# Norm products, a router constant and the first gathers in a two-layer hybrid trunk with experts

## What is computed

```python
sh1, sc1, ga1, sh2, sc2, ga2 = adaln(c, w_mod[l], b_mod[l])
p = modulated_norm(xs, g_norm1[l], sh1, sc1) @ w_in[l]
...
xs = xs + ga1 * (jnp.concatenate([out_a, out_b, out_c], axis=-1) @ w_out[l])
xs = xs + ga2 * hierarchical_moe(modulated_norm(xs, g_norm2[l], sh2, sc2), ...)
```

```python
pg = jax.nn.softmax((x @ wg) + bg, axis=-1)
pg_sel, g_sel = lax.top_k(pg, 1)
le = ((x @ we) + be).reshape(-1, N_GROUPS, EXPERTS_PER_GROUP)
le_sel = jnp.take_along_axis(le, g_sel[:, :, None], axis=1)[:, 0]
w_top, i_top = lax.top_k(jax.nn.softmax(le_sel, axis=-1), TOP_K)
...
hid = jax.nn.silu(jnp.einsum('nd,edf->nef', x, w1)) * jnp.einsum('nd,edf->nef', x, w3)
y = jnp.einsum('nef,efd->nd', hid * gates[:, :, None], w2)
```

## Time and profile before

| | |
|---|---|
| Median of 3 runs | 2230.29 us (2224.9 to 2230.62) |
| Profiled execution | 2219.47 us, span 2217.3 us |
| PE busy | 1915.4 us, 86% of the span |
| DVE, ACT, POOL busy | 896.2, 481.3, 373.1 us |
| Mean granted clock of PE | 0.918 |
| HBM read and written | 235.09 MB, 67.05 MB |

### The profile page before, as it was taken

The page is one execution under the profiler, slowest core; times in us unless marked ns, Lnnn a source line. Parts: engine busy times, 40 slices in busy tenths (PEclk is TensorE's granted clock), DMA queues, the critical chain, the costliest instruction groups (busy, mean ns, idle before and its releaser), DMA issues. The chain is left out here.

```text
span 2217.3 us, 24642 instructions
## 1 busy us (share of the span) xinstructions
PE 1915.4 (86%) x9669; PEld 1300.0 (59%) x9669; DVE 896.2 (40%) x1686; ACT 481.3 (22%) x810; POOL 373.1 (17%) x280
## 2 busy tenths in 40 slices
PE   3899978978888895899679999888888889599975
PEld 2455655558888754444345566556888865444433
DVE  2179014565555424011237920546555541311114
ACT  1211013351111213122131101344111120322212
POOL 0001150043433102100111000005444300300001
PEclk8999897999999997899789999899999999699996
DMA  9322896800000003999562112530000000499953
GB/s 358 41 75 82 278 290 209 298 1 1 1 1 1 10 2 129 354 364 365 218 161 76 38 57 77 197 126 1 1 1 1 1 12 0 168 383 358 372 226 121
DMA packets 113920, 302.54 MB, mean 136 GB/s; under 512 B 27904, under 2 KB 35746, under 8 KB 100642
## 3 DMA queue, kind: packets, MB, share of 16 engines
q1 hardware_dynamic: 65424, 218.73, 26.7%
q0 software_dynamic: 14080, 53.48, 7.3%
q10 hardware_dynamic: 34322, 28.99, 4.6%
HBM read 235.09 MB, written 67.05 MB: 136 GB/s over the span
## 5 line engine op out<-in xcount | busy, mean ns | idle before, releaser
L626 PE MATMUL ps<-hreg,ring 128*128 128x512 f32 x768 | 400.2, 603 | 7.7 <-ACT hreg L1141 7.7
L627 PEld LDWEIGHTS ps<-hreg,ring 128*128 128x128 f32 x768 | 147.8, 192 | 187.6 <-issue 187.6
L986 PE MATMUL ps<-ring,tok 128*128 128x512 f32 x544 | 237.9, 595 | 0.2 <-issue 0.2
L986 PEld LDWEIGHTS ps<-ring,tok 128*128 128x128 f32 x544 | 103.9, 191 | 130.9 <-issue 130.9
L627 PE MATMUL ps<-hreg,ring 128*128 128x128 f32 x768 | 149.0, 276 | 0.0
L1969 POOL TENSOR_TENSOR hreg<-hreg,cst 128x512 f32<-128x512 f32 x70 | 88.9, 1270 | 301.7 <-DVE hreg L1674 254.7
L1001 PE MATMUL ps<-ring,work 128*128 128x512 f32 x272 | 123.7, 598 | 0.0
L626 PEld LDWEIGHTS ps<-hreg,ring 128*128 128x128 f32 x768 | 118.8, 195 | 8.0 <-issue 8.0
L1881 DVE TENSOR_TENSOR work<-work,ps 128x256 f32<-128x256 f32 x34 | 14.2, 421 | 252.5 <-ACT work L1364 252.5
L1503 DVE SCALAR_TENSOR_TENSOR mixA<-cin_reg,small,mixA 128x655 f32<-128x655 f32 x120 | 107.0, 895 | 0.0
L1687 DVE TENSOR_TENSOR hreg<-hreg,ps 128x512 f32<-128x512 f32 x50 | 34.3, 687 | 164.9 <-PE ps L846 164.9
(11 more groups left out here) (358 smaller groups left out, 3306.5 us busy)
## 6 DMA issues: line engine op xcount, KB each, us to landing
ring<-in_w SPq DMA_DIRECT2D x102, 1024.0 KB, 8.2
ring<-in_w_mod SPq DMA_DIRECT2D x24, 2048.0 KB, 8.6
ring<-in_w_in SPq DMA_DIRECT2D x12, 2048.0 KB, 9.0
ys<-zs ACTq DMA_DIRECT2D x34, 512.0 KB, 7.8
tok<-xs SPq DMA_DIRECT2D x30, 512.0 KB, 11.0
xs<-zero POOLq DMA_DIRECT2D x8, 1792.0 KB, 19.6
ys<-zero POOLq DMA_DIRECT2D x8, 1664.0 KB, 18.6
ring<-in_w_out SPq DMA_DIRECT2D x4, 2048.0 KB, 8.1
```

What stands on the lines that cost most here:

```text
L626: mm(o[:, 0:TS], lhs(k), rhs(k)[:, 0:TS], start=k == 0, stop=k == nk - 1)
L627: ins = mm(o[:, TS:T], lhs(k), rhs(k)[:, TS:T], start=k == 0, stop=k == nk - 1)
L986: ins = mm(bank(2 + q), xgT[q][:, k, :], w, start=k == 0, stop=k == KD - 1)
```

## The change

It does five things.

- POOL multiplies four slices of the second norm (k = 4 to 7) and DVE the other four (k = 0 to 3), all right after `lrow`; ACT takes k in plain order.
- The two constant rows are spread over 128 partitions beforehand: two matmuls behind slice m = 2 of the out projection, two DVE copies at m = 3 into `crb`. The five matmuls that added the row go; DVE's copy of the logits becomes an add.
- SP waits for gather 1 (`xf_loaded[1]`) before it issues the weights of block 1's expert, and so before all that follows on its queue.
- POOL issues gathers 2 and 3 ahead of the ten scatters.
- The turn of block 1 goes to banks 4 and 5, and no longer waits for the copy of block 0.

```diff
-        norm_x = signal("norm_x", KD + 2)
-        norm_xp = signal("norm_xp", KD - 2)
+        norm_x = signal("norm_x", KD + 4)
+        norm_xp = signal("norm_xp", KD - 4)
...
                 need(blocks_ready, 1)
+                need(xf_loaded[1], 16)
                 sp.sem_inc(once["turns"], 1)
...
+                    if m == 2:
+                        need(logit_copied, 1)
+                        for g_ in range(2):
+                            ins = mm(ps[:, 2940 + 20 * g_:2960 + 20 * g_], ident[0:2, g_:g_ + 1].to_broadcast([2, P]), crow,
+                                     start=True, stop=True)
+                        ins.then_inc(logit_rows.sem, 1)
...
-                    mm(o, lrow[:, P * t:P * (t + 1)], route_c[:, X_SEL:X_SEL + 20], start=True, stop=False)
-                    ins = mm(o, ident[0:2, g_:g_ + 1].to_broadcast([2, P]), crow, start=False, stop=True)
+                    ins = mm(o, lrow[:, P * t:P * (t + 1)], route_c[:, X_SEL:X_SEL + 20], start=True, stop=True)
...
                 turn_block(0)
-                need(xg_copied, 1)
                 need(xf_loaded[1], 16)
-                turn_block(1)
+                turn_block(1, 2048)
...
-                    for k in range(KD) if n == 0 else (0, 2, 3, 4, 1, 5, 6, 7):
+                    for k in range(KD):
...
-                        elif k < 2:
+                        elif k < 4:
                             need(norm_x, KD + k + 1)
...
-                copy_tokens(0, 1)
+                copy_tokens(0, 1, 2048)
...
+                    if m == 3:
+                        need(logit_rows, 2)
+                        V.tensor_copy(crb[:, 0:4, :], ps[:, 2940:2960].rearrange("p (a n) -> p a n", a=1).to_broadcast([P, 4, 20]))
+                        step(V.tensor_copy(crb[:, 4, :], ps[:, 2960:2980]))
...
-                norm_one(0)
+                for k in range(4):
+                    norm_one(k)
...
-                step(V.tensor_copy(lr, ps[:, 2048:2148].rearrange("p (c n) -> p c n", c=NCH)))
+                step(V.tensor_tensor(lr, ps[:, 2048:2148].rearrange("p (c n) -> p c n", c=NCH), crb, ALU.add))
...
-                norm_one(1)
...
-                for k in range(2, KD):
+                for k in range(4, KD):
                     G.tensor_tensor(hT[:, k, :], xT[:, k, :], rst, ALU.mult).then_inc(norm_xp.sem, 1)
...
                 first_rows_of(0)
                 first_rows_of(1)
+                settle(xg_turned, 1)
+                first_rows_of(2)
+                settle(xg_turned, 2)
+                first_rows_of(3)
                 for c_ in range(NCH):
...
-                settle(xg_turned, 1)
-                first_rows_of(2)
-                settle(xg_turned, 2)
-                first_rows_of(3)
```

More of the change, by code:

```diff
@@ L72 @@
 PRM_DMAS = 17
-ACT_STEPS, DVE_STEPS, POOL_STEPS = 17, 234, 1
+ACT_STEPS, DVE_STEPS, POOL_STEPS = 17, 235, 1
 R_BMOD, R_G1, R_G2, R_CW, R_CB = 0, 48, 56, 64, 126
@@ L212, in build @@
         crow = work[0:2, 512:532]
+        crb = work[:, 752:852].rearrange("p (c n) -> p c n", c=NCH)
         route_c = work[:, 544:544 + NX]
@@ L397, in build @@
         mixc_ready = signal("mixc_ready", 4)
-        logit_rows = signal("logit_rows", 2)
+        logit_rows = signal("logit_rows", 3)
         logit_copied = signal("logit_copied", 2)
@@ L936, in _ @@
                     o = ps[:, 2048 + 20 * t:2068 + 20 * t]
-                    g_ = 0 if t < TS // P else 1
-                    mm(o, lrow[:, P * t:P * (t + 1)], route_c[:, X_SEL:X_SEL + 20], start=True, stop=False)
-                    ins = mm(o, ident[0:2, g_:g_ + 1].to_broadcast([2, P]), crow, start=False, stop=True)
+                    ins = mm(o, lrow[:, P * t:P * (t + 1)], route_c[:, X_SEL:X_SEL + 20], start=True, stop=True)
                 ins.then_inc(logits.sem, 1)
@@ L964, in _, with turn_block @@
                 ins.then_inc(ranks.sem, 1)
-                def turn_block(q):
+                def turn_block(q, a=0):
                     for k in range(KD):
-                        ins = turn(ps[:, P * k:P * (k + 1)], xg[q].rearrange("p (m k) -> p k m", k=KD)[:, k], ident)
+                        ins = turn(ps[:, a + P * k:a + P * (k + 1)], xg[q].rearrange("p (m k) -> p k m", k=KD)[:, k], ident)
                     ins.then_inc(xg_turned.sem, 1)
@@ L1132, in norm @@
                     sh = 24 * n
-                    for k in range(KD) if n == 0 else (0, 2, 3, 4, 1, 5, 6, 7):
+                    for k in range(KD):
                         if n == 0:
                             need(norm_x, k + 1)
-                        elif k < 2:
+                        elif k < 4:
                             need(norm_x, KD + k + 1)
                         else:
-                            need(norm_xp, k - 1)
+                            need(norm_xp, k - 3)
                         A_(hT[:, k, 0:TS], hT[:, k, 0:TS], ACT.Identity, scale=A[n][:, k, 0:1], bias=mod[:, sh + k, 0:1])
@@ L1351, in wait, with copy_tokens @@
                     act.wait_ge(sig.sem, sig.at(l, base) + pr * step)
-                def copy_tokens(pr, q):
+                def copy_tokens(pr, q, a=0):
                     wait(pr, xg_turned, q + 1, 2)
-                    A_(xgT[q], ps[:, 0:D].rearrange("p (k n) -> p k n", k=KD), ACT.Copy).then_inc(xg_copied.sem, 1)
+                    A_(xgT[q], ps[:, a:a + D].rearrange("p (k n) -> p k n", k=KD), ACT.Copy).then_inc(xg_copied.sem, 1)
                 def store(pr, q):
@@ L1767, in _ @@
                 need(norm_r, 2)
-                need(logit_rows, 2)
+                need(logit_rows, 3)
                 V.tensor_tensor(lrow, ps[:, 3072:3072 + T], rst, ALU.mult).then_inc(logit_copied.sem, 1)
-                norm_one(0)
+                for k in range(4):
+                    norm_one(k)
                 def r(a, n):
```

## The result

The changed kernel took 2238.16 us (median of 10 runs, 2230.05 to 2242.61), the kernel before 2230.26 us in as many runs (2220.31 to 2233.4). The ratio is 1.0037 with a 95% interval of 1.0019 to 1.0054: slower by some 8 us (4 to 12), where 4.7 had been forecast. So everything here is read inside the stage, from the first product of the router's logits with `wrA` (`t0`: 842.36 and 1888.46 before, 842.88 and 1904.46 after) to the first result of pair 1 (DVE's copy into `zs`), which lies behind every wait of the loop's start.

A forecast was written before the change was run, and what follows sets the result against it. PE bounds the loop from pair 1 on; pair 1's start hangs on ring 0's reload, released when the scatters land. Terms -2.3 (layer 0), +2.6 (layer 1), +4.4 (cold starts) sum to +4.7: 2235.0 us, range 2224 to 2245.

The forecast's parts named there:

- release: SP's first reload of ring 0, allowed once all ten scatters have landed: forecast at 911.6 and 1959.2.
- Cold start: PE at a lower clock after each new wait before pair 1: 2.2 us per layer, +4.4 in all.
- the same 9.4 million bytes: Bytes to pass between the weights' issue and SP's release, so later weights (+8.0) put the release off equally.
- +6.5: Delay of SP's release per layer: 8.0 from later weights, less 1.5 for the transfers' cleaner start.
- the prediction's own signs that the forecast falls: SP's release at most 3 us later than before, pair 1 starting without a wait, or later pairs waiting for weights.
- PE would have wanted pair 1 at 886.7 + 28.5 = 915.2: Layer 0: PE ready for pair 1 at 915.2, then waiting 5 us for ring 0, ready at 920.1.
- rival C (ports share): VectorE's products not held up by POOL, or gathers landing in 3 us: 2228.5 us; chance 0.20.
- the 2.0: Front of each layer, norm products and spread row: turns of hT, hx stores and gathers 2.0 us earlier.
- Rival E: Gathers take 9 us even alone, weights and release come 13 later: +15, 2245 us; chance 0.05.
- -2.3 for ring 0: Layer 0's pair 1: ring 0 ready at 920.1 against the old start of 922.38, 2.3 us earlier.
- Rival D: Forecast's mechanism, scatters gating the reload, with upper prices for release, ys stores and cold starts: +10, 2240 us; chance 0.22.
- D's own sign: SP's release coming later than 912.5 in layer 0 and 1961 in layer 1.

The follow-up runs named there:

- a_gate: Changed kernel with SP's wait for the ten scatters moved from before the pair loop to before each load of tokens from xs: 2239.98 us, ratio to before 1.0054.
- only_gathers: Kernel before with only SP's wait for gather 1, gathers 2 and 3 ahead of the scatters, and the second turn's other banks: 2242.05 us, ratio 1.0067.
- a_nosp: Changed kernel without SP's wait for gather 1, so block 1's weights go out ahead of the gathers again: 2232.8 us, ratio to before 1.0025.
- a_scatter: Changed kernel with gathers 2 and 3 behind the ten scatters again, SP's wait for gather 1 kept: 2220.02 us, ratio to before 0.9978.
- a_params: Changed kernel with ScalarE's 17 loads of the next layer's parameters moved behind the expert loop: 2238.99 us, ratio to before 1.0061.
- c_gp: Changed kernel with the edits of a_gate and a_params together, gathers 2 and 3 still ahead of the scatters: 2224.61 us, ratio to before 0.9993.
- only_products: Kernel before with only the norm products four and four and the constant row spread beforehand: 2223.43 us, ratio 0.9993.
- c_all: Changed kernel with the edits of a_gate, a_params and a_scatter together: 2241.23 us, ratio to before 1.0068.

## Why the prediction was right, and where it was not

**The direction and its cause in layer 1 were right, near to the number.** The scatters gate the reload, the reload moves back, pair 1 starts later although pair 0 starts much earlier. Forecast after `t0` in layer 1: release 70.7, measured 71.7. From the release to ring 0's use 7.3 was forecast, with 1.25 more for the stores of ys, and 7.4 measured: the stores were issued at 1968.06, 8 us ahead of the release, and cost nothing there. Start of pair 1 against before: +2.6 forecast, +2.4 measured. Cold start: 2.2 forecast, 2.8 measured. Together 4.8 forecast and 5.2 measured. a_gate shows the cause by taking the wait away (8.2 us less in that layer), only_gathers by making it without the rest.

**The order of gathers and scatters was judged too mildly.** The prediction moved the release with the weights alone, "the same 9.4 million bytes", and took 1.5 off. a_nosp and a_scatter show how the delay is made up: with SP's wait gone the release is 2.4 earlier in layer 1, with the scatters in front again it is 6.4 earlier. The sum came out close (71.7 for 70.7), but its term was named wrongly: not the weights' date but the scatters' does most of it. That its +6.5 met a measured 7.4 (8.5 in layer 0) is in part luck.

**Layer 0 was wrong in its mechanism.** Forecast: pair 1 starts 2.3 earlier, behind a wait of 5 us for ring 0, and pays 2.2 for a cold start, in sum -0.1. Measured: no wait for ring 0 at all, 9.53 us for ScalarE, and +3.8 (2.9 against the mean of the three profiles of before). That pair 1 starts without a wait was one of the prediction's own signs that the forecast falls, and in layer 0 it came. The step that failed is "PE would have wanted pair 1 at 886.7 + 28.5 = 915.2": it took pair 0's own length as fixed. That length held 14.0 us of ScalarE's DMA issues and a wait of 2.94 for them, which the timeline of before shows, and I never costed these when the change moved the last two loads into the full stretch: 24.7 us. Pair 0 took 40.8 (885.93 to 926.74). There was a second gate close in front of that start: with the first opened (a_params) ring 0 let pair 1 go only 3.2 us earlier, 9.5 behind the release. c_gp opens both. The 2.2 for a cold pair 1 in layer 0 wasn't paid either: its products ran in 13.90. What ran cold was pair 0's second half, 12.1 from 914.60 to pair 1, and 10.9 before.

**The front.** Products: forecast one each 2.12 and the fourth's end at 14.5 after `t0`; measured 7.75 for four and 14.4 (857.28 in layer 0). Turns of hT: 22.5 forecast, 22.2 measured. Alone a product takes VectorE 0.82 and POOL 1.49, in all 9.2 for four of each; side by side they took from 848.84 to 857.28, 8.4. So the engines hold each other up nearly whole, as the rule says that the prediction cites from the Trainium skill ("SBUF — State Buffer", Who interferes with whom), and rival C (ports share) is out. The front as a whole gave more than the 2.0: the turns of hT start 2.6 earlier after `t0` in layer 0, and the first gather is issued 2.7 and 3.5 earlier. What was added to the out projection cost more than the +0.2: from its first product on `dnT` to `t0` it takes 66.4 in layer 0 where it took 65.7 in all three profiles of before, 0.7.

**Gathers.** Forecast 4.05 from the end of gather 1's issue. Gather 0 was turned 3.5 after the end of its issue in layer 0 and gather 1, for which PE waited 0.38, 4.5 (879.64 to 884.17, from 878.68 with 0.96): right. Rival E is out. a_nosp shows what held the gathers up before: with the weights ahead of it again, gather 0 is turned 8.1 after the end of its issue in layer 1, and 3.5 in the changed kernel. Pair 0's products started 8.5 and 10.7 earlier, not 7.2 and 7.9. Block 1's weights were late by 2.95 in layer 0 and 0.38 in layer 1, where 1 to 3 had been forecast.

**The sum.** +3.8 and +5.2 in the profiles make 9.0; against the mean of the three profiles of before it is 7.8, and the runs say 8. The forecast was 4.7, and the missing part is layer 0, whose -0.1 was the sum of two terms that were both not there (-2.3 for ring 0 and +2.2 cold). Rival D (+10) was nearer in size. Of its upper prices a part was paid: the release came 2.0 (layer 0) and 1.0 (layer 1) later than forecast, which in layer 0 is past D's own sign, and the cold start cost 2.8 of its 3.6. But the stores of ys cost nothing, and what made layer 0 slow was ScalarE's queue, which D doesn't have.

**What stays open.** For some kernels time and stage don't agree: only_products gained 10 us in its two stages against the mean of before, but 1.6 (with up to 5 in the interval) in the runs, c_gp the same, and a_scatter more in the runs than in the stage. a_params, c_all and c_gp, the three kernels with the parameter loads behind the loop, are all 7 to 9 us worse in the runs than in the stage, of which 2 to 3 lie behind the loop, as a_params shows; but only_products, which leaves the loads where they were, is 8 worse, too. Every kernel but before has one profile, and the unchanged stretch from pair 1 of layer 0 to the next `t0` moves by 9 us between three profiles of before alone; I can't tell an effect of the edits there from that spread.

## What to carry to other kernels

A wait put on a queue delays all that stands behind it, and an engine that issues DMAs is itself such a queue: before moving a transfer, list for each consumer which transfers are ahead of its own, and for each issuing engine what it must still issue while the transfers are full. Starting earlier gains nothing where the next stage is released by something that was moved back; the gate to look for is the one behind the stage that you speed up. If a stage has several gates close together, opening one shows only the next, so open them together before judging, and look at what the freed transfers now overtake (c_all opened all three and lost).

## What the runs showed of the hardware

Issuing a DMA can cost the engine far more than the 0.3 to 0.5 us that most issues of these loads took: the load of 64 KB from `w_in`, in pieces of 64 bytes, held ScalarE for 1.22 us in the kernel before (160 GB/s moved meanwhile), 10.44 in the changed kernel (404 GB/s) and 19.10 in a_gate (409 GB/s from 899 to 919). That full transfers are what holds such an issue fits all these runs, but no run changes the transfers alone.

Stages with no changed line took different lengths in different executions of the same program: 222.5 or 225.8 us for the next layer's projection, 947.5 to 956.6 for the whole stretch between the two stages, which is more than most of the effects studied here. One profile of each kernel would have charged nearly 12 us of that to the change.
